# Sample attention in steps of three: a sequence's two page halves, then its caches, with the first two steps' pages loaded one stage earlier

## The chip, the cores and the metric

The program runs on one core of a Trainium2 chip. The metric is the device time of one execution in microseconds (us), here the median of three runs. Engines are named as in the profile: PE (TensorE, the matmuls), PEld (its weight loads), DVE (VectorE), ACT (ScalarE), POOL (GpSimd) and SP (SyncE). SP and POOL issue the transfers of the stages looked at here. A line such as L1074 is a line of the kernel before.

## What is computed

One layer of a hybrid decoder, for 1024 prompt rows and for 8 sequences of 8 new tokens each. The new tokens attend in two ways, and this part is what the change touches:

```python
def sample_layer(x, kva_bufs, kvb_pool, page_table, conv_buf, lw):
    ...
    for g in range(N_GROUPS):                       # windows (128,1), (512,4), (2048,16)
        buf = kva_bufs[g]
        ...
        full = jnp.concatenate([buf.astype(new_rows.dtype), new_rows], axis=1)
        groups.append((full[:, :, 0], full[:, :, 1], lg + jnp.arange(Sd, dtype=jnp.int32)))
    o_a = dilated_mixture(qa, groups)               # softmax over the cached window rows
    past = kvb_pool[page_table].reshape(B, past_len, 2, H_B, HEAD_DIM)
    full_b = jnp.concatenate([past.astype(new_kvb.dtype), new_kvb], axis=1)
    o_b = stick_breaking_block(qb, pos, full_b[:, :, 0], full_b[:, :, 1], k_pos, sb_bias)
```

Stick-breaking weighs key s by sigmoid(z_s) times the product of (1 - sigmoid(z_j)) over the later keys j, in log space: a suffix sum. It reads 32 pages of 128 rows for each sequence (keys and values, 256 KB a page), through a page table. The dilated part reads three window caches, 13 blocks of 128 rows for each sequence.

## The kernel before

The program is a chain of stages, each a block in which every engine runs its own instruction list, joined by semaphores: norm, input projection, dilated attention of the prompt, stick-breaking of the prompt (`prompt_stick_stage`), `sample_stage`, projections, FFN, final norm. Between two blocks all engines meet.

`sample_stage` runs 24 steps. Steps 0 to 15 are **stick steps**, two for each sequence: half 1 and half 0 of its pages, 16 pages each. Steps 16 to 23 are **cache steps**, one for each sequence, 13 blocks. Pages and caches land in four slots of 16 blocks. `load_pages` issues them: SP the groups 0 and 1 of each step, POOL the groups 2 and 3. A page costs a register load from the table and one transfer of 256 KB; a cache group is one transfer of up to 1 MB. The load for step k waits until step k-4 has used its slot (`v_done`).

SP's list in this stage: the page table, the 64 new rows (into `kt`, named `rows`), bias, sb_bias, two masks `own` and `own01`, `new_v`, fold, after, same, mask, three small `vnew` loads, and then its page loads. DVE's list begins with a wait for `own_in` (the last of its four transfers is `new_v`), after which a chain over DVE, ACT and PE prepares the new tokens' rows (`new_rows` on PE). PE turns the first page only behind that chain.

A step k in the list of PE: `turn(k+1)` (transposes of the next step's key blocks into the bank `tbank`, copied out to `kt` by ACT and DVE in turns), a small matmul (`carry`, or `turn_maxima` in a cache step), `turn_weights(k)`, `scores(k+1)`, in some steps a turn-out of a finished sequence (`turn_out` for stick results, L1485 and L1487, or `turn_out_shared` for cache results, L1495 and L1496), and `values(k)` (L1458), which needs `awT`, DVE's copy of the turned weights (`move_weights`, L1282). The results of a turn-out lie in the bank `xbank`; DVE puts them in their place by `place` (four small copies, L1300) or `place_shared` (a reciprocal, L1304, and four products, L1309).

Where these stand decides the waits. In the stick steps 3, 5, ... 15 PE has a `turn_out` between `scores(k+1)` and `values(k)`, and DVE has `read_out(k-1)`, which waits for it, `carried`, `place` and only then `move_weights(k)`. In the other stick steps there is none. In the cache steps DVE's `move_weights` stands ahead of `place` and `place_shared`. The order is written out by hand.

Of the kernel before, what the change touches and what calls it, by code (L numbers as in the profile page):

```python
# [20 lines left out]
P = 128  # L21
# [19 lines left out]
EPS = 1e-6  # L41
Z_MAX = 41.0
# [739 lines left out]
def prompt_stick_stage(nc, K, a, zs, oTd, extra_pool):  # L782


    with stage(nc, "ps") as s:
# [38 lines left out]
        @block.sync  # L824
        def _(sp):
            sp.dma_start(strict[:, :], a["strict"]).then_inc(small_in, 16)
            sp.dma_start(bias[:, :], a["sb_bias"].partition_broadcast(P)).then_inc(small_in, 16)
            for t in range(QT):
                sp.dma_start(rows[:, t, :], zs[t * P:t * P + P, QB:ZC]).then_inc(row_in[t], 16)
            sp.wait_ge(o_done, N)  # L830
            sp.dma_start(oTd[:, 2:4, 0:SEQ], oT[:, :, :]).then_inc(o_stored, 16)
            sp.wait_ge(o_stored, 16)

        @block.gpsimd
        def _(pool):
            for t in range(QT):
                pool.wait_ge(row_in[t], 16)
            extra_pool(pool)
# [171 lines left out]
def sample_stage(nc, K, a, zs, oTd):  # L1010


    with stage(nc, "sm") as s:
        C = 4 * NS
        HALF = PAGES // 2
        SLOTS = 4
        STICK = 2 * NB
        STEPS = STICK + NB
        ROUNDS = STEPS // SLOTS
        pages = s.sb("pages", [P, SLOTS * HALF, 512])  # L1020
        table = s.sb("table", [1, NB * PAGES], I32)
# [10 lines left out]
        out = s.sb("out", [P, 2, 256])  # L1032
# [10 lines left out]
        page_in = [[s.sem(f"page_in{u}{g}") for g in range(4)] for u in range(SLOTS)]  # L1043
        rows_in, table_in, small_in, own_in, vnew_in = (s.sem(n) for n in ("rows_in", "table_in", "small_in", "own_in", "vnew_in"))
# [13 lines left out]

        def landed(k, g):

            return sum(64 if i < STICK else 16 for i in range(k % SLOTS, k + 1, SLOTS))

        def load_pages(eng, groups):

            for k in range(STEPS):
                u = k % SLOTS
                if k >= SLOTS:
                    eng.wait_ge(v_done, k - SLOTS + 1)
                for g in groups:
                    if k < STICK:  # L1070
                        b, first = k // 2, HALF * (1 - k % 2)
                        with eng.Fori(0, 4) as j:
                            page = eng.value_load(table[0:1, ds(j + (b * PAGES + first + 4 * g), 1)], min_val=0, max_val=NPOOL - 1)
                            eng.dma_start(pages[:, ds(j + (u * HALF + 4 * g), 1), :],  # L1074
                                          a["pool"][ds(page, 1), :, :].rearrange("a p c -> p a c")).then_inc(page_in[u][g], 16)
                    else:
                        b = k - STICK
                        src = (a["cache2"][b].rearrange("(k r) c -> k r c", r=4),
                               a["cache3"][b].rearrange("(k r) c -> k r c", r=16)[:, 0:4, :],
                               a["cache3"][b].rearrange("(k r) c -> k r c", r=16)[:, 4:8, :],  # L1080
                               a["cache1"][b].unsqueeze(1))[g]
                        first = u * HALF + 4 * g
                        eng.dma_start(pages[:, first:first + (4 if g < 3 else 1), :], src).then_inc(page_in[u][g], 16)

        @block.sync
        def _(sp):
            sp.dma_start(table[:, :], a["page_table"]).then_inc(table_in, 16)
            sp.dma_start(rows[:, 0:ZC], zs[SEQ:ROWS, :]).then_inc(rows_in, 16)
            sp.dma_start(bias[:, :], a["stick_bias"]).then_inc(small_in, 16)
# [11 lines left out]
            sp.wait_ge(table_in, 16)  # L1101
            load_pages(sp, (0, 1))
# [6 lines left out]
        def _(pool):  # L1109
            pool.wait_ge(table_in, 16)  # L1110
            load_pages(pool, (2, 3))

        def move(eng, k, e):

            u = e % 2
            n = 512 if k < STICK or e < 6 else P
# [10 lines left out]
        def _(act):  # L1127
# [11 lines left out]
            for k in range(STEPS):  # L1139
                u, more = k % 2, k + 1 < STEPS  # L1140
                if k < STICK:
# [4 lines left out]
                    act.wait_ge(odds_done, k + 1)  # L1146
                    if k >= 2:
                        act.wait_ge(scanned, k - 1)
                    act.activation(soft[:, u, :], odds[:, u, :], ACT.Ln, bias=1.0).then_inc(soft_done, 1)
                    if more:  # L1150
                        move(act, k + 1, 2)
                    act.wait_ge(scanned, k + 1)
                    if k >= 2:
                        act.wait_ge(a_done, k - 1)
                    act.activation(left[:, u, :], suffix[:, u, :], ACT.Exp, scale=-1.0).then_inc(left_done, 1)
# [3 lines left out]
                    act.wait_ge(nbias_done, k + 1)  # L1159
                    act.wait_ge(o_done, max(0, k - 1))  # L1160
                    act.activation(factor[:, u:u + 1], nbias[:, u:u + 1], ACT.Exp).then_inc(factor_done, 1)
                else:
                    if more:
                        move(act, k + 1, 0)
                    act.wait_ge(nm_done, k - STICK + 1)
                    if k >= STICK + 2:
                        act.wait_ge(share_done, k - STICK - 1)
                    act.activation(odds[:, u, :], odds[:, u, :], ACT.Exp, bias=nm[:, u:u + 1], scale=SCALE,
# [855 lines left out]
```

## Time and profile before

| what | us |
| --- | --- |
| runs | 2311.25, 2316.29, 2320.03 (median 2316.29) |
| the profiled execution | 2309.15, of which its span 2307.6 |
| prompt stick-breaking, last transfer issued | 850.55 |
| sample stage, SP's first transfer issued | 855.49 |
| sample stage, first page turned on PE | 880.03 |
| sample stage, SP's first store issued | 1194.34 |

Over the whole span PE is busy 85%, DVE 42%, ACT 25%, POOL 5%. The stage of interest is some 340 us of 2308. In a timeline row the columns are: start, length, engine, line, operation, what it writes <- what it reads, shapes, count, and in brackets how long the engine sat idle before it and what released it. In a windows row they are: the stretch and its length, then for each engine its busy time with the number of instructions, and last the clock granted to TensorE (1.00 is 2.4 GHz, 0.50 is 1.2 GHz), the mean busy share of the 16 DMA engines, and GB/s.

### The profile page before, as it was taken

To read this page: it belongs to the slowest core of one execution; us is meant where nothing else is said; L and a number is where in the kernel's file an instruction comes from. 1 tells how busy PE (TensorE), PEld (TensorE's weight loads), DVE (VectorE), ACT (ScalarE), POOL (GpSimd) and SP (SyncE) were. 2 spreads that over 40 slices of the span, in tenths; PEclk is the share of its full clock that TensorE was granted. 3 is DMA by queue.
4 is the path that set the end of the run, shared out by engine and by line. 5 is a ranking of instruction groups with operands and counts; after the bars stand their busy time and mean duration, and the time that the engine had idled before them with its cause. 6 is when DMAs were issued, how large, how long until landed. Compare 5 with 4: busy or idle time off the path is not lost. (4 is left out here: it accounts for less than half of the span.)

```text
span 2307.6 us, 32275 instructions
## 1 busy us (share of the span) xinstructions
PE 1952.0 (85%) x11654; PEld 1644.0 (71%) x11654; DVE 978.0 (42%) x1841; ACT 587.2 (25%) x948; POOL 114.9 (5%) x208
## 2 busy tenths in 40 slices
PE   2799999998776747787867695799999999999984
PEld 2577888998444534555647584799999999999973
DVE  3344100000464844445436414345545455555554
ACT  3101111111754642233211103222221222122212
POOL 0000000000201003331000000000000000000000
PEclk9899999999878777999988797899999999999997
DMA  2844455111826129998633400311110111101102
GB/s 93 325 153 154 153 206 197 55 48 57 229 48 206 38 55 345 343 318 317 258 132 124 180 1 10 89 39 55 55 36 18 55 55 40 45 24 55 36 16 86
DMA packets 132446, 273.96 MB, mean 119 GB/s; under 512 B 23225, under 2 KB 74826, under 8 KB 128330
## 3 DMA queue, kind: packets, MB, share of 16 engines
q1 hardware_dynamic: 110890, 153.93, 20.0%
q0 software_dynamic: 21472, 118.91, 14.6%
q8 instruction: 53, 0.87, 0.2%
q14 instruction: 31, 0.25, 0.0%
HBM read 243.37 MB, written 79.10 MB: 140 GB/s over the span
## 5 line engine op out<-in xcount | busy, mean ns | idle before, releaser
L447 PE MATMUL ff_ups<-act_hi,ff_up_hi 128*128 128x364 f32 (+1 forms) x1056 | 234.1, 330 | 14.8 <-DVE ff_up_lo L1786 14.8
L447 PE MATMUL ff_ups<-act_lo,ff_up_hi 128*128 128x364 f32 (+1 forms) x1056 | 233.8, 330 | 0.0
L447 PE MATMUL ff_ups<-act_hi,ff_up_lo 128*128 128x364 f32 (+1 forms) x1056 | 233.8, 330 | 0.0
L1837 DVE TENSOR_TENSOR act_x<-act_x,ff_dps 128x512 f32<-128x512 f32 (+1 forms) x198 | 135.9, 686 | 216.1 <-PE ff_dps L1888 216.1
L447 PEld LDWEIGHTS ff_ups<-act_hi,ff_up_hi 128*128 128x128 f32 x1056 | 184.4, 189 | 16.5 <-DVE ff_up_lo L1786 15.0
L422 PE MATMUL inp_ps<-inp_w_hi,h_hi 128*128 (+1 forms) x432 | 170.5, 395 | 22.8 <-DVE inp_w_lo L381 20.9
L447 PEld LDWEIGHTS ff_ups<-act_lo,ff_up_hi 128*128 128x128 f32 x1056 | 184.0, 189 | 0.0
L447 PEld LDWEIGHTS ff_ups<-act_hi,ff_up_lo 128*128 128x128 f32 x1056 | 184.0, 189 | 0.0
L422 PE MATMUL inp_ps<-inp_w_lo,h_hi 128*128 (+1 forms) x432 | 170.0, 393 | 0.0
L422 PE MATMUL inp_ps<-inp_w_hi,h_lo 128*128 (+1 forms) x432 | 169.6, 393 | 0.0
L1888 PE MATMUL ff_dps<-ff_dn_hi,ff_f_hi 128*128 128x512 f32 (+1 forms) x396 | 158.0, 399 | 9.3 <-DVE ff_f_lo L1827 9.3
L1888 PE MATMUL ff_dps<-ff_dn_lo,ff_f_hi 128*128 128x512 f32 (+1 forms) x396 | 157.8, 398 | 0.0
L1888 PE MATMUL ff_dps<-ff_dn_hi,ff_f_lo 128*128 128x512 f32 (+1 forms) x396 | 157.6, 398 | 0.0
L381 DVE TENSOR_TENSOR inp_w_lo<-inp_raw,inp_w_hi (+1 forms) x10 | 44.3, 4425 | 252.3 <-ACT inp_w_hi L347 252.3
L1382 PE MATMUL sm_tbank<-all_ident,sm_pages 128*128 128x128 f32 x720 | 115.7, 299 | 35.6 <-ACT sm_kt L1122 15.9
L1382 PEld LDWEIGHTS sm_tbank<-all_ident,sm_pages 128*128 128x128 f32 x720 | 83.5, 150 | 74.4 <-issue 42.5
L422 PEld LDWEIGHTS inp_ps<-inp_w_hi,h_hi 128*128 128x128 f32 (+1 forms) x432 | 79.5, 184 | 43.3 <-issue 23.4
L1743 ACT ACTIVATE ff_c<-ff_ups,ff_cb,ff_cw 128x728 f32<-128x728 f32 x44 | 42.3, 961 | 260.5 <-PE ff_ups L447 260.5
L1756 ACT ACTIVATE ff_f_hi<-ff_c 128x1088 fp32r<-128x1088 f32 x22 | 24.5, 1114 | 305.6 <-DVE ff_c L1825 305.6
L1124 DVE COPY sm_kt<-sm_tbank 128x512 f32<-128x512 f32 x96 | 62.9, 655 | 89.2 <-PE sm_tbank L1382 89.1
L422 PEld LDWEIGHTS inp_ps<-inp_w_hi,h_lo 128*128 128x128 f32 (+1 forms) x432 | 79.6, 184 | 20.0
L422 PEld LDWEIGHTS inp_ps<-inp_w_lo,h_hi 128*128 128x128 f32 (+1 forms) x432 | 79.7, 184 | 19.8
(250 smaller groups left out, 3200.3 us busy)
## 6 DMA issues: line engine op xcount, KB each, us to landing
sm_pages<-in_pool POOLq DMA_DIRECT2D x128, 256.0 KB, 4.8
sm_pages<-in_pool SPq DMA_DIRECT2D x128, 256.0 KB, 4.6
out_s<-in_cache POOLq DMA_DIRECT2D x8, 4080.0 KB, 20.9
ff_up_raw<-in_w_up SPq DMA_DIRECT2D x44, 512.0 KB, 4.7
inp_raw<-in_w_in POOLq DMA_DIRECT2D x10, 2048.0 KB, 9.4
sm_pages<-in_cache SPq DMA_DIRECT2D x16, 1024.0 KB, 9.5
zs<-inp_zt SPq DMA_DIRECT2D x48, 256.0 KB, 4.5
ff_dn_raw<-in_w_down SPq DMA_DIRECT2D x22, 512.0 KB, 4.4
```

The source lines that it names most:

```text
L381: dve.tensor_tensor(w_lo[:, c % 2, :, :], raw[:, c % 2, :, :], w_hi[:, c % 2, :, :].bitcast(F32), ALU.subtract).then_inc(lo_done, 1)
L422: last = pe.matmul(zbank[t % 3][0:n, :], h[:, k, t * P:t * P + n], w[:, c % 2, k, :], start=(i == 0), stop=(i == 3 * KD - 1))
L447: last = pe.matmul(out[:, n * 512:n * 512 + b - a], lhs, rhs[:, a:b], start=(i == 0), stop=(i == len(pairs) - 1))
L1124: eng.tensor_copy(dst, src).then_inc(moved[1], 1)
L1382: last = pe.transpose(tbank[:, hp * 512 + j * P:hp * 512 + j * P + P], pages[:, k % SLOTS * HALF + 4 * g + j, hp * P:hp * P + P], K["ident ...
L1743: act.activation(pieces(c[:, k, 0:FRONT]), front(u), ACT.Identity, bias=cb[:, ds(j + k * FT, 1)], scale=cw[:, 2, ds(j + k * FT, 1)]).then_ ...
L1756: act.activation(f_hi[:, u, :], c[:, 1, :], ACT.Copy).then_inc(f_hi_done, 1)
L1837: dve.tensor_tensor(x, x, dps[0:n, k * 512:k * 512 + 512], ALU.add).then_inc(added, 1)
L1888: last = pe.matmul(dps[0:n, k * 512:k * 512 + 512], x[:, u, t * P:t * P + n], w[:, u, k * 512:k * 512 + 512], start=(q == 0), stop=(q == 5))
```

## The change

The 24 steps are put in another order: step 3b and 3b+1 are the two page halves of sequence b, step 3b+2 its caches. All indices follow (`stick(k)` counts stick steps). `load_pages` becomes a function of its own. The first half of the slots and the page table are allocated ahead of the prompt's stick-breaking stage, and that stage's SP and POOL issue the loads of steps 0 and 1, once its own rows are in; on POOL they stand ahead of the cache copies (`extra_pool`). In the sample stage SP issues the loads of steps 2 and 3 directly behind the new rows, ahead of the small loads. `out` has three slots instead of two. `place(b-1)` and `place_shared(b-1)` run in the stick steps 3b and 3b+1, ahead of `move_weights(k)`, and `turn_out(b-1)` and `turn_out_shared(b-1)` in the same two steps on PE.

```diff
 def prompt_stick_stage(...): sp
             for t in range(QT):
                 sp.dma_start(rows[:, t, :], zs[t * P:t * P + P, QB:ZC]).then_inc(row_in[t], 16)
+            sp.dma_start(G["table"][:, :], a["page_table"]).then_inc(G["table_in"], 16)
+            sp.wait_ge(row_in[QT - 1], 16)
+            sp.wait_ge(G["table_in"], 16)
+            load_pages(sp, G, a, (0, 1), 0, 2)
             sp.wait_ge(o_done, N)
...
             for t in range(QT):
                 pool.wait_ge(row_in[t], 16)
+            pool.wait_ge(G["table_in"], 16)
+            load_pages(pool, G, a, (2, 3), 0, 2)
             extra_pool(pool)
...
 def sample_stage(...): sp
-            sp.dma_start(table[:, :], a["page_table"]).then_inc(table_in, 16)
             sp.dma_start(rows[:, 0:ZC], zs[SEQ:ROWS, :]).then_inc(rows_in, 16)
+            load_pages(sp, G, a, (0, 1), 2, SLOTS)
             sp.dma_start(bias[:, :], a["stick_bias"]).then_inc(small_in, 16)
...
-            sp.wait_ge(table_in, 16)
-            load_pages(sp, (0, 1))
+            load_pages(sp, G, a, (0, 1), SLOTS, STEPS, v_done)
...
             def read_out(k):
...
-                dve.wait_ge(x_ready, min(k // 2, NB) + max(0, k - STICK - 1))
+                if b:
+                    dve.wait_ge(x_ready, 2 * b - 1 if is_stick(k) else 2 * b)
...
                     carried(k)
-                    if k % 2 == 1 and k >= 3:
-                        place(k // 2 - 1)
+                    if k >= 3:
+                        (place if k % 3 == 0 else place_shared)(k // 3 - 1)
                     move_weights(k)
...
                     tops(k)
                     move_weights(k)
-                    if k == STICK:
-                        place(NB - 1)
-                    if k >= STICK + 2:
-                        place_shared(k - STICK - 2)
                     peaks(k)
...
                 if k + 1 < STEPS:
                     scores(k + 1)
-                if k < STICK:
-                    if k % 2 == 1 and k >= 3:
-                        turn_out(k // 2 - 1)
-                else:
-                    if k == STICK:
-                        turn_out(NB - 1)
-                    if k >= STICK + 2:
-                        turn_out_shared(k - STICK - 2)
+                if k >= 3 and is_stick(k):
+                    (turn_out if k % 3 == 0 else turn_out_shared)(k // 3 - 1)
+                if not is_stick(k):
                     spread_tops(k)
+                if k + 1 == STEPS:
+                    turn_out(NB - 1)
                 values(k)
```

SP at the start of the sample stage, before (`sm_kt` is where the new rows land; the page loads begin behind mask and vnew).

```order
L1087 DMA sm_table<-in_page_table 1x256
L1088 DMA sm_kt<-zs 64x3072
L1089 DMA sm_bias<-in_stick_bias 128x1
L1090 DMA sm_bias4<-in_sb_bias 128x4
L1091 DMA sm_own<-in_own 64x256
L1092 DMA sm_own01<-in_own01 64x256
L1093 DMA sm_new_v<-zs 64x256
L1094 DMA sm_fold<-in_fold 128x32
```

The same place with the change. The load of a page is the body of a loop that runs four times, and the loop stands there twice, for groups 0 and 1.

```order
L1102 DMA sm_kt<-zs 64x3072
L1037 DMA sm_pages<-in_cache2 128x2048
L1037 DMA sm_pages<-in_cache3 128x2048
...
L1028 TENSOR_LOAD pg_table
...
L1029 DMA sm_pages<-in_pool 128x512
...
L1104 DMA sm_bias<-in_stick_bias 128x1
L1105 DMA sm_bias4<-in_sb_bias 128x4
L1106 DMA sm_own<-in_own 64x256
L1107 DMA sm_own01<-in_own01 64x256
L1108 DMA sm_new_v<-zs 64x256
```

Two 1 MB and eight 256 KB transfers, the eight with a register load each, now stand ahead of bias, own and new_v.

DVE from one step's last copy to `kt` to the next step's first, in two successive stick steps before: one with `place` ahead of the copy to `awT`, one without.

```order
L1124 COPY sm_kt<-sm_tbank 128x512 x2
L1292 TENSOR_SCALAR sm_out<-sm_obank,sm_factor 128x256
L1244 SCALAR_TENSOR_TENSOR sm_nbias<-sm_ybank,sm_total 128x1
L1300 COPY sm_oT<-sm_xbank 64x8 x4
L1282 COPY sm_awT<-sm_abank 128x512
L1221 TENSOR_SCALAR sm_odds<-sm_zbank,sm_bias_z 128x512
...
L1244 SCALAR_TENSOR_TENSOR sm_nbias<-sm_ybank,sm_total 128x1
L1282 COPY sm_awT<-sm_abank 128x512
```

The same with the change, in the two stick steps of a sequence.

```order
L1314 TENSOR_TENSOR sm_share<-sm_den,sm_factor 128x1
L1315 TENSOR_SCALAR sm_out<-sm_obank,sm_factor 128x256
L1262 SCALAR_TENSOR_TENSOR sm_nbias<-sm_ybank,sm_total 128x1
L1323 COPY sm_oT<-sm_xbank 64x8 x4
L1303 COPY sm_awT<-sm_abank 128x512
L1239 TENSOR_SCALAR sm_odds<-sm_zbank,sm_bias_z 128x512
...
L1262 SCALAR_TENSOR_TENSOR sm_nbias<-sm_ybank,sm_total 128x1
L1327 RECIPROCAL sm_parts<-sm_xbank 128x32
L1332 TENSOR_TENSOR sm_oT_a<-sm_xbank,sm_parts 64x8 x4
L1303 COPY sm_awT<-sm_abank 128x512
```

Both stick steps of a sequence now have work on `xbank` ahead of the copy to `awT`: 14 steps (3, 4, 6, 7, ... 21, 22) where it was 7.

## Rows read from the trace of the kernel before

**Rows 1.** Windows, two stretches of the sample stage: first page turned to step 15, then cache steps.

```profile
880.00:1077.00 197.00, 157.57 (x1338) 103.24 (x1338) 96.05 (x168) 60.82 (x116) 62.23 (x116) 0.92 0.95 331
1077.00:1195.00 118.00, 100.31 (x1222) 69.03 (x1214) 57.17 (x168) 29.82 (x68) 7.43 (x14) 0.98 0.52 204
```

**Rows 2.** Waits, 880 to 1075 us: engine, tile, line, releaser: total us, times, longest.

```profile
PE sm_tbank L1382 <- DMA sm_pages<-in_pool: 6.4, 4, 2.3
```

**Rows 3.** Timeline, start, first turned page, first values and end of the sample stage.

```profile
855.86 0.50 SPq L1088 DMA_DIRECT2D sm_kt<-zs  x1
858.68 0.60 SPq L1093 DMA_DIRECT2D sm_new_v<-zs  x1
863.92 0.18 DVE L1182 COPY sm_bias_c<-sm_bias 128x32 f32<-128x32 f32 x1 [6.16 <-DMA sm_new_v<-zs]
880.03 6.36 PE L1382 MATMUL sm_tbank<-all_ident,sm_pages 128*128 128x128 f32 x28 [0.26 <-DVE sm_total L1211]
...
899.08 1.94 PE L1458 MATMUL sm_obank<-sm_pages,sm_awT 128*32 128x256 f32 x32
...
1193.56 0.75 DVE L1309 TENSOR_TENSOR sm_oT_a<-sm_xbank,sm_parts 64x8 f32<-64x8 f32 x4
```

**Rows 4.** Timeline, SP's first page loads.

```profile
863.99 7.96 SPq L1074 DMA_DIRECT2D sm_pages<-in_pool  x6
```

**Rows 5.** DMA issues by line: count, KB each, median us from issue to landing.

```profile
sm_pages<-in_cache SPq DMA_DIRECT2D x16, 1024.0 KB, 9.5
```

**Rows 6.** Timeline of PE, stick steps 7 and 8 (values of 6, 7, 8).

```profile
979.03 1.94 PE L1458 MATMUL sm_obank<-sm_pages,sm_awT 128*32 128x256 f32 x32
980.89 1.09 PE L1382 MATMUL sm_tbank<-all_ident,sm_pages 128*128 128x128 f32 x8
...
988.19 1.92 PE L1395 MATMUL sm_zbank<-sm_kt,sm_qpad 128*32 128x512 f32 x16
...
991.27 0.63 PE L1487 MATMUL sm_xbank<-sm_fold,sm_out 128*128 128x32 f32 x4
994.12 2.73 PE L1458 MATMUL sm_obank<-sm_pages,sm_awT 128*32 128x256 f32 x32 [2.21 <-DVE sm_awT L1282]
...
1006.24 1.94 PE L1458 MATMUL sm_obank<-sm_pages,sm_awT 128*32 128x256 f32 x32
```

**Rows 7.** Values of line 1458: idle time before them, us and times.

```profile
  DVE sm_awT L1282: 15.5, 7
```

**Rows 8.** Timeline of DVE, end of step 7: from the turn-out's landing to awT.

```profile
992.05 0.48 DVE L1292 TENSOR_SCALAR sm_out<-sm_obank,sm_factor 128x256 f32<-128x256 f32 x1 [3.96 <-PE sm_xbank L1487]
...
992.51 0.74 DVE L1300 COPY sm_oT<-sm_xbank 64x8 f32<-64x8 f32 x4
993.28 0.69 DVE L1282 COPY sm_awT<-sm_abank 128x512 f32<-128x512 f32 x1
```

**Rows 9.** Timeline of DVE, `place_shared` in a cache step.

```profile
1148.24 0.36 DVE L1304 RECIPROCAL sm_parts<-sm_xbank 128x32 f32<-128x32 f32 x1 [1.76 <-PE sm_xbank L1496]
1148.63 0.75 DVE L1309 TENSOR_TENSOR sm_oT_a<-sm_xbank,sm_parts 64x8 f32<-64x8 f32 x4
```

**Rows 10.** Timeline of PE, a cache step: values, turn of the next, turn-out.

```profile
1148.44 2.07 PE L1458 MATMUL sm_obank<-sm_pages,sm_awT 128*32 128x256 f32 x32
...
1151.09 1.09 PE L1382 MATMUL sm_tbank<-all_ident,sm_pages 128*128 128x128 f32 x8
...
1156.01 0.27 PE L1435 MATMUL sm_ybank<-all_ident,sm_mx 128*1 128x128 f32 x1
...
1159.33 0.39 PE L1496 MATMUL sm_xbank<-sm_fold,sm_share 128*128 128x32 f32 x2
...
1159.95 2.07 PE L1458 MATMUL sm_obank<-sm_pages,sm_awT 128*32 128x256 f32 x32
```

**Rows 11.** Windows around step 7's wait for awT: ahead of it, just behind it.

```profile
980.00:992.00 12.00, 10.20 (x88) 6.70 (x80) 4.56 (x7) 3.95 (x7) 4.23 (x8) 1.00 0.98 352
995.00:998.00 3.00, 3.00 (x26) 1.90 (x19) 0.00 (x0) 0.07 (x1) 0.48 (x1) 0.52 0.91 303
```

More of the change, by code:

```diff
@@ L41 @@
 EPS = 1e-6
+SLOTS = 4
 Z_MAX = 41.0
@@ L1007, in _, with load_pages, sample_stage @@
                     values(it - 1, turns[it - 1] - 1)
-def sample_stage(nc, K, a, zs, oTd):
+def load_pages(eng, G, a, groups, first, last, consumed=None):
+    for k in range(first, last):
+        u, half = k % SLOTS, k % 2 * (PAGES // 2)
+        pages = G["pages"][u // 2]
+        if k >= SLOTS:
+            eng.wait_ge(consumed, k - SLOTS + 1)
+        for g in groups:
+            if k % 3 < 2:
+                at = k // 3 * PAGES + PAGES // 2 * (1 - k % 3) + 4 * g
+                with eng.Fori(0, 4) as j:
+                    page = eng.value_load(G["table"][0:1, ds(j + at, 1)], min_val=0, max_val=NPOOL - 1)
+                    eng.dma_start(pages[:, ds(j + (half + 4 * g), 1), :],
+                                  a["pool"][ds(page, 1), :, :].rearrange("a p c -> p a c")).then_inc(G["page_in"][u][g], 16)
+            else:
+                b = k // 3
+                src = (a["cache2"][b].rearrange("(k r) c -> k r c", r=4),
+                       a["cache3"][b].rearrange("(k r) c -> k r c", r=16)[:, 0:4, :],
+                       a["cache3"][b].rearrange("(k r) c -> k r c", r=16)[:, 4:8, :],
+                       a["cache1"][b].unsqueeze(1))[g]
+                eng.dma_start(pages[:, half + 4 * g:half + 4 * g + (4 if g < 3 else 1), :], src).then_inc(G["page_in"][u][g], 16)
+def sample_stage(nc, K, G, a, zs, oTd):
     with stage(nc, "sm") as s:
@@ L1057, in sample_stage, with is_stick, stick, page @@
         block = s.ctx.enter_context(nc.Block())
+        def is_stick(k):
+            return k % 3 < 2
+        def stick(k):
+            return k // 3 * 2 + k % 3
         def landed(k, g):
[L1061 to L1069, printed above, removed]
-                    if k < STICK:
[L1071 to L1075, printed above, removed]
-                    else:
[L1077 to L1083, printed above, removed]
+            return sum(64 if is_stick(i) else 16 for i in range(k % SLOTS, k + 1, SLOTS))
+        def page(k, i):
+            return G["pages"][k % SLOTS // 2][:, k % 2 * HALF + i, :]
         @block.sync
         def _(sp):
-            sp.dma_start(table[:, :], a["page_table"]).then_inc(table_in, 16)
             sp.dma_start(rows[:, 0:ZC], zs[SEQ:ROWS, :]).then_inc(rows_in, 16)
+            load_pages(sp, G, a, (0, 1), 2, SLOTS)
             sp.dma_start(bias[:, :], a["stick_bias"]).then_inc(small_in, 16)
@@ L1140, in _ @@
                 u, more = k % 2, k + 1 < STEPS
-                if k < STICK:
+                if is_stick(k):
+                    m = stick(k)
+                    v = m % 2
                     if more:
@@ L1459, in add @@
                                      tile_position=(row, C * g), skip_group_check=True)
-                if k < STICK:
+                if is_stick(k):
                     for j in range(4):
                         for g in range(4):
-                            last = add(g, awT[:, u, j, C * g:C * g + C], pages[:, page + 4 * g + j, 256:512], j == 0, j == 3)
+                            last = add(g, awT[:, u, j, C * g:C * g + C], page(k, 4 * g + j)[:, 256:512], j == 0, j == 3)
                 else:
-                    if k == STICK:
+                    b = k // 3
+                    if b == 0:
                         pe.wait_ge(vnew_in, 48)
@@ L1955, in program @@
         prompt_dilated_stage(nc, K, a, o, zs, scratch["ls"], oTd)
-        prompt_stick_stage(nc, K, a, zs, oTd, lambda pool: copy_caches(pool, a, o, copied, (0, 1)))
-        sample_stage(nc, K, a, zs, oTd)
+        with ExitStack() as c1:
+            s1 = Store(nc, c1, "pg")
+            G = {"pages": [s1.sb("pages", [P, PAGES, 512])], "table": s1.sb("table", [1, NB * PAGES], I32), "table_in": s1.sem("table_in"),
+                 "page_in": [[s1.sem(f"page_in{u}{g}") for g in range(4)] for u in range(SLOTS)]}
+            prompt_stick_stage(nc, K, G, a, zs, oTd, lambda pool: copy_caches(pool, a, o, copied, (0, 1)))
+            sample_stage(nc, K, G, a, zs, oTd)
         with ExitStack() as c1:
```

192 lines of the change are left out of this document (95 added, 97 removed).

## The prediction

> **What bounds the kernel now.** I read the windows of the sample stage first, since the change lies there. While page halves are worked on, the DMA engines are 95% busy at 331 GB/s; in the cache steps they are half idle (52%, 204 GB/s) [rows 1]. Read alone, this speaks for mixing the two kinds of step. The waits say otherwise: in that first stretch of 197 us PE waited for a page 4 times, 6.4 us in all [rows 2]. A full DMA queue is not yet a late one. The timeline of PE shows what sets the pace: values, turn, scores, turn-out and values again follow with small gaps, 979.03 to 994.12 to 1006.24 [rows 6]. The rest is PE's own list and the copies that it waits for.
>
> The start must be read next, as the change loads two steps ahead of it. SP issues the new rows at 855.86 and new_v at 858.68; DVE goes on at 863.92, released by new_v; the chain behind it ends at 880.03, when PE turns the first page, released by DVE's copy of the totals and not by a page [rows 3]. So **the first step's pages were in time already**. Loading them earlier gives PE nothing. What counts at the start is when new_v lands.
>
> **Part 1: the loads issued a stage earlier.** They go out after that stage's own rows are in; SP's next work there is the store at the stage's end, and POOL's only other work is the cache copies, which nobody awaits until the program's end. 32 page transfers of 256 KB are 8.4 MB, 25 us at 331 GB/s [rows 1], inside a stage with over 100 us left (850.55 is its last transfer). I cost them at nothing; if they disturbed it, a few us.
>
> **Part 2: the small loads behind the loads of steps 2 and 3.** SP's page loads come at (7.96 - 0.35) / 5 = 1.52 us apart, six in 7.96 us [rows 4] (0.35 is about one issue's own time). Ahead of new_v there are now eight of them, 12.2 us, and two cache transfers, some 0.4 us each, less the page table's, which has gone (0.37): it is issued about **12.6 us later**, at 871.3 instead of 858.68 [rows 3]. Then it must land, which took 863.92 - 858.68 = 5.2 us [rows 3]. Now SP and POOL have put the loads of steps 2 and 3 into the queues from 857 on, 3.4 MB of caches and 4.2 MB of pages, all issued by 870; at 331 GB/s [rows 1] these 7.6 MB drain at 857 + 23 = 880. A 1 MB cache transfer, issued together with others, landed after 9.5 us [rows 5], which from 871.3 gives 880.8. If new_v lands only behind SP's own loads, DVE goes on at about 880.5: **+16.6 us**. Bounds: +12.6 if it passes them all, +21 if the small ones ahead of it add 4 us. I take 16.6, since more than half of the backlog (4.2 of 7.6 MB) is on SP's own queue. The chain behind it keeps its 880.03 - 863.92 = 16.1 us; mask, fold and same are needed only 12 us into it. PE starts to turn at 896.6.
>
> The Trainium skill, page "DMA: Bandwidth & Descriptors", section "Queues, rings and completion order", says that a DMA engine takes turns between the queues it has work for and takes the descriptors of one queue in order. By that rule a small transfer on SP's queue cannot pass SP's pages, whatever POOL has queued, which is the 16.6; by overtaking the sum would be 4.0 us less. No row of the trace before has a small transfer behind a backlog.
>
> While PE waits, all four slots are full, so the DMA engines stand idle from 880 until step 0's values free one, at 896.6 + 19.05 (899.08 - 880.03, [rows 3]) = 915.6. They have time to spare, see below.
>
> **Part 3: place ahead of awT in 14 steps instead of 7.** In step 7 the turn-out ends at 991.90 and values start at 994.12: PE sat idle 2.21 us because DVE, released by the turn-out, did out, nbias, place and awT first [rows 6, 8]. This is paid 7 times, 15.5 us [rows 7]. With the change read_out asks for an older turn-out, so out and nbias (992.05 to 992.51, 0.46) go ahead of it: a wait of 2.21 - 0.46 = 1.75 in the first stick step of each sequence. In the second, place_shared takes 1148.24 to about 1149.40, 1.16 us, instead of place's 993.28 - 992.51 = 0.77 [rows 8, 9]: 1.75 + 0.39 = 2.14. Seven of each: 7 x 1.75 + 7 x 2.14 = 27.2. Less 15.5: **+11.7 us**. In the cache steps PE did not wait for place_shared before, since awT stood ahead of it: its values start at 1159.95 right behind the turn-out [rows 10], so nothing comes back there.
>
> **Part 4: the turn of page halves in cache steps.** PE's matmuls are the same in number and shape, only in another order. In a cache step, the turn of 13 blocks took 1156.01 - 1151.09 = 4.9 us for 26 transposes [rows 10]; in a stick step 32 of them with carry and weights took 988.19 - 980.89 = 7.3 [rows 6]. The sums over the stage stay as they were within about **+1.5 us** (the last copy to kt of a half now has only the turned weights of a cache step to hide behind, 0.2 us in 7 steps). The bounds are 0 and 3.
>
> **Part 5: waits for pages.** These 6.4 us [rows 2] go: **-6.4 us** at most, -3 where they hid other gaps. A sequence asks for 2 x 4.2 + 3.4 = 11.8 MB in three steps. PE needs for these, by [rows 6, 10], 15.1 + 14 + 10.4, some 39.5 us; the transfers need 11.8 MB / 331 GB/s = 35.6 us. So pages stay in time, with a small margin.
>
> **Part 6: TensorE's clock.** Behind step 7's wait the granted clock was 0.52 (1.2 GHz), against 1.00 ahead of it, and values took 2.73 us instead of 1.94 [rows 6, 11]. From there to the next values it is 1006.24 - 994.12 = 12.1 us, where the parts at full clock give 1.86 (values) + 7.30 (turn and weights) + 1.9 (scores) = 11.1 [rows 6]: a fall costs about 1.1 us. The mean clock of that stretch, 0.92, means half speed for 16% of 197 us [rows 1]; looked at in windows of 2 us, five of the 7 waits have such a spell right behind them. I take the same share of 14, 10 falls, 5 more: **+5.5 us**. Bounds: -5.5 if the shorter waits trip nothing, +9.9 if each does.
>
> The page "TensorE: Matmul & The Clock Gate", section "A second HAM failure mode: psum-queue depth-cycling", of the Trainium skill describes short idle times between groups of matmuls that are frequent enough to make the clock go back and forth. The rows agree at 2.21 us of idle; by that rule doubling such gaps costs the 5.5, without it the sum would be 5.5 less.
>
> **The sum.** 16.6 + 11.7 + 1.5 - 6.4 + 5.5 = **+28.9 us**, slower. On the profiled execution, 2309.15, that is 2338.1. This execution was 7.1 us below the median of the runs, 2316.29; against the median it is 2345.2, and I say 2345. The unknown terms at their low ends: 12.6 + 11.7 + 0 - 6.4 - 5.5 = +12.4; at their high ends 21 + 11.7 + 3 - 3 + 9.9 = +42.6.
>
> **Rivals.** (a) **Pages are the bound after all**, and the result is faster. If the pace of the stick steps follows the traffic (95% busy, [rows 1]) and PE's small gaps hide it, then taking 8.4 MB out of the stage saves 25 us and spreading the rest fills the idle half of the cache steps; with the start's loss of 16.6 and 11.7 of Part 3 hidden in the slack, the time is some 2292 to 2305. It decides from the point where PE's waits for pages exceed the 29 us of the other terms; against it stand the 6.4 us [rows 2]. (b) **new_v does not wait**, and the clock does not fall more often: +12 or a little less, 2324 to 2329; within 0.5% if DVE, which starts its next step right behind awT, gives back part of Part 3. For it: the transfer is small; against it: 12.6 us of issue alone are sure. (c) **Pages run late**: cache transfers of 1 MB and pages share three steps of 39.5 us with 35.6 us of transfers. If the rate falls to 300 GB/s, these need 39.4, and waits of 1 to 3 us in each of 7 sequences come on top: 2355 to 2366. (d) **The early loads do not run early**: POOL or SP issue them late in the prompt's stage. Since the first turn waits for the chain and not for pages, this changes nothing.
>
> **How the numbers follow.** Forecast, +18 to +40: 0.68. (b) 0.16, half of it within 0.5% of the time before. (c) 0.08. (a) 0.08, three quarters of it faster by over 0.5%. 0.5%, 11.6 us, is about what a measurement of this kernel can tell from no change. So faster 0.06, within 0.5% 0.11, slower 0.83. The range of 8 in 10 goes from 2324 (the low ends together, 2328.7, and 4 for the spread of the runs) to 2361 (the high ends together, 2358.9, and part of (c)).
>
> **What would show it.** In the timeline after: DVE's bias_c released by new_v at about 880 instead of 863.9; the first turn 16 us behind that, released by DVE; a DMA share near nothing between 880 and 915. In the idle times ahead of values: 14 waits for awT, 27 us. In the waits: none of note for pages. In the windows: clock falls behind most of the 14. Wrong would be: new_v landed by 872; a stage shorter than 339 us; long waits of PE for pages, which would be (c).

## The result

The changed kernel takes 2361.93 us (median of 4 runs, 2359.70 to 2364.09); beside it the kernel before took 2314.62 (4 runs, 2311.25 to 2320.03). The ratio is 1.0202, interval 1.0178 to 1.0226: 2% slower. The direction was forecast, the size was not: 2345 was said, with a range up to 2361, and the measured time lies just above that.

### The profile after

The profiled execution took 2364.09 us, its span 2362.6: 55.0 more than before. Windows of the sample stage after: from SP's first transfer to the end of the chain that prepares the new rows, then from there to SP's first store. The columns are those of [rows 1].

```profile
858.81:901.25 42.44, 8.62 (x38) 6.30 (x38) 8.84 (x27) 2.95 (x5) 5.42 (x10) 0.50 0.64 217
901.25:1251.39 350.14, 280.62 (x2552) 175.50 (x2552) 153.76 (x337) 90.36 (x184) 63.41 (x118) 0.89 0.64 225
```

The same two stretches of the kernel before:

```profile
855.49:879.81 24.32, 8.62 (x38) 6.30 (x38) 8.85 (x27) 2.95 (x5) 7.79 (x14) 0.50 0.98 291
879.81:1194.34 314.53, 257.88 (x2552) 172.27 (x2552) 153.38 (x337) 90.64 (x184) 69.66 (x130) 0.94 0.79 284
```

I call the first the start, the second the compute stretch. They account for the 55.0 us:

| where | before | after | us |
| --- | --- | --- | --- |
| up to the prompt stage's last transfer | 850.55 | 853.81 | +3.3 |
| start | 24.32 | 42.44 | +18.1 |
| compute stretch, PE busy | 257.88 | 280.62 | +22.7 |
| compute stretch, PE idle | 56.65 | 69.52 | +12.9 |
| the rest | | | -2.0 |

The largest row is not a wait. PE ran the same 2552 matmuls in both and was busy with them 22.7 us longer, at a granted clock of 0.89 instead of 0.94. At half speed for a share s of a stretch the mean clock is 1 - s/2, so 0.89 means some 77 us at 1.2 GHz of the 350, and 0.94 some 38 us of the 315 (counted in windows of 1 us: 77 in 22 spells, and 35 in 9).

The +3.3 is not shown to come from the change. Of all thirteen kernels profiled, the ten with the early loads issued that last transfer between 849.6 and 856.2, the three without (before, e5, e7) at 850.6 to 852.2.

**The start.** SP after; answers to the first two rows of [rows 3]:

```profile
858.81 0.53 SPq L1102 DMA_DIRECT2D sm_kt<-zs  x1
861.45 10.84 SPq L1029 DMA_DIRECT2D sm_pages<-in_pool  x8
875.61 1.62 SPq L1108 DMA_DIRECT2D sm_new_v<-zs  x1
```

DVE after, in the same stretch:

```profile
885.36 0.18 DVE L1200 COPY sm_bias_c<-sm_bias 128x32 f32<-128x32 f32 x1 [24.28 <-DMA sm_new_v<-zs]
901.25 0.17 DVE L1229 COPY sm_total<-sm_ybank 128x8 f32<-128x8 f32 x1 [3.60 <-PE sm_ybank L1387]
```

new_v is issued 16.8 us behind SP's first transfer, where it was 3.2 ([rows 3] and the table ahead of the prediction), and lands 885.36 - 875.61 = 9.8 us later instead of 5.2. PE waits with DVE: it is idle 23.5 us ahead of its first matmul behind this, where it was 4.9.

**The compute stretch.** What PE's values waited for after, which answers to [rows 7]:

```profile
  DVE sm_awT L1303: 25.9, 14
```

PE after: the values of a sequence's first stick step, then its second, in which the blocks of the cache step are turned and scored:

```profile
1042.92 3.57 PE L1478 MATMUL sm_obank<-pg_pages,sm_awT 128*32 128x256 f32 x32 [1.66 <-DVE sm_awT L1303]
1046.42 1.09 PE L1401 MATMUL sm_tbank<-all_ident,sm_pages 128*128 128x128 f32 x8
...
1050.79 0.96 PE L1401 MATMUL sm_tbank<-all_ident,sm_pages 128*128 128x128 f32 x5 [0.64 <-DVE sm_kt L1137]
1052.23 0.33 PE L1401 MATMUL sm_tbank<-all_ident,sm_pages 128*128 128x128 f32 x1 [0.48 <-DVE sm_kt L1137]
...
1053.92 1.08 PE L1422 MATMUL sm_zbank<-sm_kt,sm_qpad 128*32 128x256 f32 x8
```

Windows over the same stretch:

```profile
1039.00:1043.00 4.00, 2.34 (x23) 1.74 (x20) 1.57 (x6) 0.00 (x0) 1.61 (x3) 0.98 1.02 343
1043.00:1046.50 3.50, 3.50 (x33) 1.58 (x34) 0.44 (x1) 0.00 (x0) 0.02 (x1) 0.53 0.74 274
1046.50:1053.00 6.50, 4.47 (x32) 3.37 (x33) 4.23 (x7) 3.63 (x7) 2.07 (x4) 1.00 0.63 193
1053.00:1056.50 3.50, 3.50 (x48) 2.13 (x50) 0.34 (x2) 0.20 (x1) 1.15 (x3) 0.52 0.89 303
```

There are two kinds of spell. The first follows a wait for awT: clock 0.53, and values take 3.57 us instead of the 1.94 of [rows 6]. The second follows no such wait. It comes at the end of the turn of a cache step's 13 blocks, whose last group has one transpose for each copy (the `x1` row) instead of four, and it lies on the scores of the caches, where one group of 8 takes 1.08 us. From the third sequence on, each has three spells of some 3.5 us. All 14 waits for awT are followed by one (values take 2.76 to 3.60 us), and 6 of the 8 thin ends. Before, 5 of the 7 waits were, though all seven lasted 2.21 us; and the second kind came once, at the change from stick to cache steps, with the same row at 1.08 us (in the other seven cache steps it took 0.61):

```profile
1096.29 1.08 PE L1404 MATMUL sm_zbank<-sm_kt,sm_qpad 128*32 128x256 f32 x8
```

The idle time of the compute stretch grew by 12.9 us. Waits for awT account for +10.4 and waits for pages for -6.4. What is left is small and frequent: waits of the turn for the copies to `kt`, 28.7 us before and 35.9 after, and short issue gaps ahead of the scores, 1.5 and 3.5 us. The waits for the copies, before and after:

```profile
PE sm_tbank L1382 <- ACT sm_kt L1122: 15.9, 46, 0.6
PE sm_tbank L1382 <- DVE sm_kt L1124: 12.8, 36, 0.6
```

```profile
PE sm_tbank L1401 <- ACT sm_kt L1135: 20.6, 53, 0.6
PE sm_tbank L1401 <- DVE sm_kt L1137: 15.3, 32, 0.6
```

### The profile page after: what moved, and what is told of

Its sections match the earlier page's. It is cut to its first block and busy times, and to the rows that moved or that the text cites. A ratio compares the mean times of both kernels' runs of the same rounds, so it can differ in the third digit from the quotient of the medians.

```text
span 2362.6 us, 32273 instructions
## 1 busy us (share of the span) xinstructions
PE 1974.9 (84%) x11654; PEld 1644.4 (70%) x11654; DVE 979.9 (41%) x1841; ACT 587.1 (25%) x948; POOL 115.1 (5%) x208
## 5 line engine op out<-in xcount | busy, mean ns | idle before, releaser
L382 DVE TENSOR_TENSOR inp_w_lo<-inp_raw,inp_w_hi (+1 forms) x10 | 44.3, 4426 | 252.4 <-ACT inp_w_hi L348 252.4
L1135 ACT ACTIVATE sm_kt<-sm_tbank 128x512 f32<-128x512 f32 x96 | 54.3, 565 | 186.7 <-PE sm_tbank L1401 186.0
L1904 PEld LDWEIGHTS ff_dps<-ff_dn_hi,ff_f_hi 128*128 128x128 f32 (+1 forms) x396 | 72.7, 184 | 29.1 <-DVE ff_f_lo L1843 9.7
```

Source lines behind the costliest of these rows:

```text
L382: dve.tensor_tensor(w_lo[:, c % 2, :, :], raw[:, c % 2, :, :], w_hi[:, c % 2, :, :].bitcast(F32), ALU.subtract).then_inc(lo_done, 1)
L1135: eng.activation(dst, src, ACT.Copy).then_inc(moved[0], 1)
L1904: last = pe.matmul(dps[0:n, k * 512:k * 512 + 512], x[:, u, t * P:t * P + n], w[:, u, k * 512:k * 512 + 512], start=(q == 0), stop=(q == 5))
```

## The experiments

The theory: three independent costs, namely the small loads behind the pages; the waits for awT with the clock falls behind them; and the clock falls at the thin end of a cache turn, now between page halves in every sequence (this third one was added after e1 to e8). Rivals: the traffic of pages and caches, the order in threes by itself, and for the clock, that more work for PE lowers it. Unless said otherwise an experiment is an edit of the changed kernel. "Start" and "compute stretch" are as above.

**e1_small_first** puts the loads of steps 2 and 3 on SP back behind the small loads.

```diff
             sp.dma_start(rows[:, 0:ZC], zs[SEQ:ROWS, :]).then_inc(rows_in, 16)
-            load_pages(sp, G, a, (0, 1), 2, SLOTS)
...
-            load_pages(sp, G, a, (0, 1), SLOTS, STEPS, v_done)
+            load_pages(sp, G, a, (0, 1), 2, STEPS, v_done)
```

> The changed kernel with one edit: SP issues the loads of steps 2 and 3 behind the small loads again. Theory (new_v behind SP's page loads, 18.1 us of the 57 that the sample stage ends later, and a term of its own): new_v lands some 5 us after its issue, the first page is turned about 24.5 us after SP's first transfer of the stage instead of 42.7, and the time falls by 16 to 19 us, to about 2344. Rival (POOL's loads of steps 2 and 3, which stay early, hold the small loads as well, or the pages of steps 2 and 3 are then late): it falls by under 8 us, with waits for pages in steps 2 and 3.

Measured: 2350.66 us, ratio to before 1.0152 (1.0130 to 1.0174). That is 11.3 less than after and short of what was expected: the start is 29.4 us, where the kernel before has 24.3. SP's new_v, issued at 859.82 with none of SP's pages ahead of it, landed 10.5 us later. The first row is DVE's, the second POOL's, which began with its share of the loads at once:

```profile
870.32 0.18 DVE L1199 COPY sm_bias_c<-sm_bias 128x32 f32<-128x32 f32 x1 [11.23 <-DMA sm_new_v<-zs]
```

```profile
857.30 1.10 POOL L1037 DMA_DIRECT2D sm_pages<-in_cache  x2 [96.26 <-POOLq L142]
```

So order on SP's own queue is one part of it, POOL's queue another.

**e6_pool_held** asks for that second part. It is e3 (below, both edits) with POOL's page loads held until new_v is in.

```diff
+            pool.wait_ge(own_in, 64)
             load_pages(pool, G, a, (2, 3), 2, STEPS, v_done)
```

> The kernel of e3, in which POOL waits for the small loads (own_in) before it loads steps 2 and 3. In e3 the small loads landed 13.6 us after SP's first transfer of the stage, before it was 8.4. Theory (POOL's two cache transfers and pages on the same DMA engines hold them): new_v lands at 8 to 9 us, and the time falls by 5 us, to about 2299. Rival (something else delays them, or steps 2 and 3 come late): no change, or waits for pages in step 2.

Measured: 2298.49 us, 0.9908 (0.9891 to 0.9924), against 2304.01 of e3. The start is 24.1 us instead of 29.4; new_v, issued at 859.68, is in at 864.64, as in the kernel before:

```profile
864.91 1.10 POOL L1037 DMA_DIRECT2D sm_pages<-in_cache  x2 [108.95 <-DMA sm_new_v<-zs]
```

POOL's loads on their own cost the start 5.3 us. e5 (below) narrows it down to the two 1 MB cache transfers at their head.

**e2_awt_first** takes away the wait for awT: DVE copies awT ahead of `place` and `place_shared`.

```diff
                     carried(k)
+                    move_weights(k)
                     if k >= 3:
                         (place if k % 3 == 0 else place_shared)(k // 3 - 1)
-                    move_weights(k)
```

> The changed kernel with one edit: DVE copies awT before place and place_shared in the stick steps. Theory A (each of the 14 waits for awT costs its 1.85 us and, behind it, a spell of half clock of about 1.65 us): the waits (25.9 us in all) go, the spells behind them go too, and the time falls by 26 + 23 = some 45 to 50 us. Theory B (the spells come from the small gaps of the turns and stay where they are): it falls by 22 to 28 us, and values still run at half clock in most of the stick steps.

Measured: 2314.83 us, 0.9991 (0.9977 to 1.0006): 47.1 less than after, the same as before. The compute stretch:

```profile
903.85:1202.43 298.58, 254.00 (x2552) 165.68 (x2552) 153.93 (x337) 90.31 (x184) 63.21 (x118) 0.96 0.74 264
```

It lost 51.6 us, 26.6 of it PE's busy time with the same 2552 matmuls, 25.0 idle time. PE never waits for awT, and the values of the stick steps run at full speed, as here:

```profile
1043.67 1.93 PE L1478 MATMUL sm_obank<-sm_pages,sm_awT 128*32 128x256 f32 x32
```

The small work of `place` or `place_shared` ahead of awT, 14 times, cost half in waiting and half in the clock behind it. Low clock fell from 77 us to 23.

**e3_both** has both edits.

> The changed kernel with both edits of the two runs before. If the terms are independent, its gain is the sum of the two: under theory A some 60 to 68 us, which is below the kernel before (about 2297); under B some 42 us, to about 2320, the kernel before within 0.5%. If one hides the other (pages then late, since PE is faster), it is less than the sum, with waits for pages.

Measured: 2304.01 us, 0.9947 (0.9928 to 0.9965): 57.9 less than after, where 11.3 + 47.1 = 58.4. By the medians the two costs add, though short of the 60 to 68 that was expected, and the close agreement is in part chance: the compute stretch was 306.6 us here and 298.6 in e2, with low clock of 41 and 23 us, though both run the same lists in it. Two of the spells in e3 lasted some 10 us each, where none in e2 did (the one at the start apart, all lasted 3 to 4). How long the clock stays low differs between near copies by so much, and what decides it there I can't say.

**e4_filler** leaves the wait and fills it: 11 transposes of the identity on PE, nobody's input, stand behind each turn-out of the stick steps. If the clock follows PE's gaps, values run at full speed though DVE is as late as before.

```diff
                 if k >= 3 and is_stick(k):
                     (turn_out if k % 3 == 0 else turn_out_shared)(k // 3 - 1)
+                    for _ in range(11):
+                        pe.transpose(tbank[:, 0:P], K["ident"][:, :], K["ident"][:, :])
```

> The changed kernel with more work for PE: in the 14 steps that have a turn-out, 11 transposes of the identity into a bank that nobody reads, 1.5 us at full clock, between the turn-out and values, where PE waits for awT. Its results are unchanged. Theory A (the wait itself makes the clock fall): PE no longer stands idle there, values run at full clock, and the time FALLS, by 14 x 1.65 = up to 23 us, although work was added. Theory B (the fall has another cause): values stay at half speed, the filler itself takes up to 3 us at half clock, and the time stays or grows by up to 15 us.

Measured: 2346.58 us, 1.0139 (1.0109 to 1.0169). **154 useless matmuls made the kernel 15.4 us faster** (by the medians; 14.6 by the ratios to the kernel before; up to 23 was expected). The same place as above, PE:

```profile
1037.83 1.40 PE L1536 MATMUL sm_tbank<-all_ident 128*128 128x128 f32 x11
1039.64 1.93 PE L1478 MATMUL sm_obank<-pg_pages,sm_awT 128*32 128x256 f32 x32 [0.42 <-DVE sm_awT L1303]
...
1049.46 1.08 PE L1422 MATMUL sm_zbank<-sm_kt,sm_qpad 128*32 128x256 f32 x8
```

The values behind the turn-out take 1.93 or 1.94 us again, 13 times of 14; the one exception (2.04 us) lies at the end of a spell of 10 us that began at a thin turn. The second kind of spell is left. So it is PE's idle time there, not the copy or the traffic, that costs the clock, and more work does not lower it. Whether the length of the gap counts or the share of busy time around it, the filler doesn't tell, since it changes both. The compute stretch:

```profile
900.67:1232.38 331.71, 279.74 (x2706) 189.09 (x2706) 153.95 (x337) 90.23 (x184) 63.21 (x118) 0.94 0.67 238
```

**e9_padded_turn** is e6 with the thin end filled: three transposes of the identity ahead of the single one in the last group of a cache step, so that each group has four again.

```diff
+                    if not is_stick(k) and g == 3:
+                        for j in range(1, 4):
+                            pe.transpose(tbank[:, hp * 512 + j * P:hp * 512 + j * P + P], K["ident"][:, :], K["ident"][:, :])
                     for j in range(4 if is_stick(k) or g < 3 else 1):
```

> The kernel of e6 (three-step order, awT first, small loads first, POOL held) with more work for PE: in the turn of a cache step's 13 blocks, whose last group has one transpose where the others have four, three transposes of the identity are added on each side, 6 x 0.14 us for each of 8 sequences, 6.7 us in all. Results are unchanged. In e2, e5 and the changed kernel a spell of half clock begins once a sequence at the end of just this turn and lies on the cache scores behind it. Theory (the thin end of this turn is what lets the clock fall, and the order in threes puts it under a stick step 8 times where it was once): low-clock time in the stage goes from some 40 us to about 20, the compute stretch loses 9 us by it and gains 2 to 7 by the added work: 0 to 8 us faster than e6's 2298.5 in spite of the work. Rival (the spells have another cause): low-clock time stays, and the time grows by 3 to 8 us.

**e11_filler_and_padded_turn** puts both fillings into the changed kernel, small loads and waits left as they are.

> The changed kernel with the filler of e4 (11 transposes in each of the 14 waits for awT) and the padding of e9 in the cache turns. Theory: the two causes of the spells are then both gone, low-clock time in the stage goes from 77 us (e4: 38) to about 20, and the time to 2338 to 2346, at or below e4's 2346.6 in spite of 6.7 us more work. Rival: low-clock time stays at e4's 38 us and the time is 3 to 7 us above e4's.

Measured, e9: 2288.40 us, 0.9886 (0.9867 to 0.9905); e6 was 2298.49 at 0.9908. By the ratios that is 5 us, with intervals that overlap; the evidence is in the profiles. Compute stretch, first e6, then e9:

```profile
880.98:1187.83 306.85, 262.29 (x2552) 170.34 (x2552) 153.85 (x337) 90.23 (x184) 63.22 (x118) 0.93 0.74 263
```

```profile
880.71:1174.18 293.47, 251.33 (x2600) 165.90 (x2600) 153.74 (x337) 90.22 (x184) 63.21 (x118) 0.99 0.78 275
```

48 matmuls more, PE busy 11.0 us less, low clock from 41 us to 7, where 20 was expected. Measured, e11: 2335.47 us, 1.0089 (1.0069 to 1.0109), 11.1 less than e4, clock 0.99 in a stretch of 319.2, low clock 5 us in one spell. So the second kind of spell is the thin turn's, and it is worth 11 us to a kernel that has it in each sequence. With both fillings the changed kernel is 26.5 us faster, although DVE is as late with awT as before; of the 25.9 us of waits for it, 8.7 are left, and PE turns the identity during the rest.

**e5_no_early_load** is e3 without the loads in the prompt's stage; SP and POOL load steps 0 and 1 in the sample stage.

> The kernel of e3 (three-step order, small loads first, awT first) without the early loads: steps 0 and 1 are loaded in the sample stage, as in the kernel before. Theory (the first page turned waits for the chain behind new_v, so early pages give nothing): within 3 us of e3's 2304.0, the chain beginning 1 to 5 us earlier since POOL then starts with pages instead of a 1 MB transfer, against 3 to 6 us of waits for pages in the first steps. Rival (the early load is worth the 25 us of traffic that it takes out of the stage, and e3 wins by it): some 15 to 25 us slower than e3, 2319 to 2329.

Measured: 2303.67 us, 0.9939 (0.9922 to 0.9956), e3's 2304.01 at 0.9947. The early loads gain e3 nothing: its compute stretch is the same within 0.4 us, and its start is 29.4 us where it is 24.1 here. One page was late:

```profile
PE sm_tbank L1398 <- DMA pg_pages<-in_pool: 3.5, 1, 3.5
```

The shorter start is instructive, since POOL is not held here. It begins with single pages and not with two cache transfers, and new_v, issued at 859.95, lands after 5.4 us:

```profile
858.82 0.56 POOL L1027 DMA_DIRECT2D pg_pages<-in_pool  x1 [127.45 <-issue]
865.35 0.23 DVE L1197 COPY sm_bias_c<-sm_bias 128x32 f32<-128x32 f32 x1 [5.95 <-DMA sm_new_v<-zs]
```

Against e6, whose start is also 24.1, the medians give the early loads 5.2 us. That is not shown: the intervals overlap, the compute stretches agree within 0.1, and the profiled executions are 0.4 us apart.

**e8_small_loads_early** is e3 with bias4, own, own01 and new_v loaded in the prompt's stage behind its pages, and POOL held by the new rows only. The question is what bounds the start next.

> The kernel of e3 with new_v, own, own01 and sb_bias loaded in the prompt's stick-breaking stage, and POOL's loads of steps 2 and 3 held until the new rows are in. Theory (the start is bound by when the chain's inputs land): DVE goes on at the landing of the new rows and their turn, about 8.5 us after SP's first transfer instead of 13.6, and the time falls by 5 us against e3, to about 2299. Rival: the chain then waits for something else, no change.

Measured: 2294.91 us, 0.9915 (0.9888 to 0.9941), not told apart from e6. DVE takes bias_c 2.2 us behind SP's first transfer, and nothing is gained on e6, because the turned new rows are next, 8.4 us behind it, as forecast:

```profile
863.12 4.02 DVE L1208 COPY sm_qpad<-sm_tbank 64x64 f32<-64x64 f32 x16 [6.08 <-PE sm_tbank L1375]
```

**e7_old_order_awt_first** and **e10_old_order_early_load** start from the kernel before, order of steps unchanged. e7 gives `out` four slots, lets read_out ask for an older turn-out, and copies awT ahead of `place`. e10 is e7 with the early loads of steps 0 and 1, and POOL held until new_v is in.

```diff
-                dve.wait_ge(x_ready, min(k // 2, NB) + max(0, k - STICK - 1))
+                dve.wait_ge(x_ready, max(0, k // 2 - 1) if k < STICK else NB + max(0, k - STICK - 1))
...
                     carried(k)
+                    move_weights(k)
                     if k % 2 == 1 and k >= 3:
                         place(k // 2 - 1)
-                    move_weights(k)
```

> The kernel before (16 stick steps, then 8 cache steps, no early loads) with the awT edit alone: out has four slots, read_out asks for an older turn-out, and awT stands ahead of place. Theory (the 7 waits of 2.21 us and the spells of half clock behind 5 of them are dead time in the old order too): 15.5 + 5 x 1.1 to 1.6 = 21 to 24 us faster than before, about 2294, and so faster than e3: the order in threes gives nothing of itself. Rival (the old order's stick steps are bound by pages at 95% DMA, once PE stops waiting for awT): waits for pages take the place of it, the gain is under 10 us, and e3 is the faster of the two.

> The kernel of e7 (old order, awT first) with the early loads of the changed kernel: steps 0 and 1 loaded in the prompt's stick-breaking stage, POOL held until the small loads are in. e7 is the one kernel here in which PE waits for pages (10.8 us in 5 waits), so here the early load may be worth something. Theory: the waits go in full or in part, the start stays at 24.2 us: 4 to 10 us faster than e7's 2290.0. Rival (the 16 stick steps in a row drain the two steps' lead, and the waits only come later; or the prompt's stage pays for it): no change, within 3 us.

Measured, e7: 2290.02 us, 0.9886 (0.9860 to 0.9912): 26 us faster than the kernel before by the ratio, where 21 to 24 were expected, and 13.6 less than e5, the nearest kernel in threes. Compute stretch of e5, then of e7, and e7's waits for pages:

```profile
881.23:1188.14 306.91, 260.39 (x2552) 170.41 (x2552) 154.09 (x337) 90.35 (x184) 69.11 (x129) 0.94 0.82 291
```

```profile
880.48:1174.86 294.38, 248.51 (x2552) 167.25 (x2552) 153.55 (x337) 90.79 (x184) 69.64 (x130) 0.97 0.83 304
...
PE sm_tbank L1382 <- DMA sm_pages<-in_pool: 10.8, 5, 2.7
```

PE is idle 46.5 us in the one and 45.9 in the other. Nearly the whole difference is busy time, 11.9 us, so what the order in threes costs is clock; that it is by the thin turns is argued from e9, where filling them gave back 11.0. The idle times are equal because two things cancel: e5 waits 7.3 us less for pages, but 5.9 more for the copies to `kt` (35.2 and 29.3) and 2.0 more in issue gaps.

Measured, e10: **2280.72 us**, 0.9856 (0.9831 to 0.9881), faster than both kernels and the fastest of the study. No wait for a page is left, and low clock is 7 us. Against e7 the compute stretch lost 7.2 us, 4.5 of it idle time: 10.8 us of page waits went, and 5.7 came back as waits for the copies to `kt` (35.0 and 29.3):

```profile
880.52:1167.71 287.19, 245.78 (x2552) 163.46 (x2552) 152.90 (x337) 90.33 (x184) 63.25 (x118) 0.99 0.77 285
```

At this clock PE's matmuls take 245.8 us in the old order; in threes (e9) 251.3 less its 48 padding matmuls, some 0.13 us each (11 took 1.40 on their own), makes 245.2. So the same work costs the same in either order. Measured from there, the kernel before loses 12 us of busy time to the clock, the changed kernel 35.

## Why the forecast was right in direction and wrong in size

**Part 1 (early loads, 0).** For the changed kernel, right: first turn behind the chain and not behind a page, and e5 equals e3. As a general statement too narrow: where PE waits for pages they take these waits away, 7.2 us of the compute stretch in e10 against e7. They did run early, from 725.9 us on, as forecast.

**Part 2 (small loads, +16.6).** 18.1 measured. Issue was 13.6 us later by the trace, not 12.6: the small issues ahead of it got slower (the one of L1106 takes 1.56 us instead of 0.49). Landing added 4.5 against 4.0. The reason given was half wrong. I took SP's own backlog as what new_v lands behind; e1 shows that POOL's alone delays it by as much, 10.5 us against 5.0 in e6, and e5, with single pages at the head of POOL's list, 5.4. The Trainium skill, page "DMA: Bandwidth & Descriptors", section "Queues, rings and completion order", has the engines take turns between queues, which I read as a small transfer passing POOL's. In e1 it did not pass them unharmed. Moving SP's loads back (e1) took 13.1 of the 18.1 off the start, holding POOL's (e6 against e3) the other 5.3.

**Part 3 (awT, +11.7).** Right: 25.9 us in 14 waits where 27.2 were forecast, +10.4.

**Part 4 (the turn in cache steps, 0 to +3).** About right in its own terms: of two kernels that wait neither for awT nor for a page, the one in the old order (e10) is idle 41.4 us in the compute stretch and the one in threes (e6) 44.6. Its mechanism was looked at for lateness only. The row of one transpose per copy was in [rows 10]'s stage of the trace and was counted as cheap; that it drops the clock when it stands in a stick step was not seen, though the kernel before shows it once, at 1094.

**Part 5 (pages, -6.4).** Right in that no wait for a page is left, but not worth 6.4: other gaps came in their place. In e10 against e7, 10.8 us of page waits were worth 4.5 of idle time, so the -3 named there was nearer. The 39.5 us that PE was said to need for a sequence don't follow from [rows 6, 10] either, which give 15.1, 12.1 and 11.5; after, a sequence took 44.3 us (from the values at 1042.92 to those at 1087.25), so the transfers had more room than said.

**Part 6 (clock, +5.5, at most +9.9) is the step that failed.** Measured +22.7 us of busy time. Two errors. First, how many: "the same share of 14" gave 10 spells instead of 5; there were 22 instead of 9, 14 of them behind the waits (5 before) and 6 behind thin turns (1 before). Each of the shorter waits (1.66 us) dropped the clock, while two of the seven of 2.21 us before had not. Second, how much: 1.1 us was read off one spell; 13 more of them cost 22.7, 1.7 each. With 77 us at half speed in place of 35, the loss should be up to half of 42, 21 us, which fits. With 22.7 for 5.5 the sum would have been +46.1 on the profiled execution, and the median at 2362. That this meets the measured 2361.93 is luck: the profiled executions are 55.0 us apart, 8.9 more, and the one before lay 7.1 below its median and the one after 2.2 above. The upper bound of +9.9 let each of the 14 waits trip the clock once and had no room for a spell elsewhere.

Between the forecast +28.9 and the measured +55.0 on the profiled executions, Part 6 is 17.2 us. The next is short gaps: of the 12.9 us of idle time, 10.4 are waits for awT and -6.4 pages, so 8.9 are gaps of PE for the copies to `kt` and for issue, where Part 4 had 1.5. The prompt stage ended 3.3 later, the start was 1.5 longer than said, awT 1.3 less, and the rest is -2.0.

**The rivals.** (a), pages as the bound, falls: taking page waits away gave 7.2 us of the compute stretch at the best (e10 against e7). (b), new_v doesn't wait, falls by the 9.8 us of landing. (c), pages late, falls: no such wait, although 2362 is in its range; by the time alone it would have looked right. (d) decides nothing, as said. The Trainium skill's "TensorE: Matmul & The Clock Gate", section "A second HAM failure mode: psum-queue depth-cycling", describes short idle times that send the clock to and fro. The trace agrees, and more strongly than I let it count: it was given +5.5 us, e2 shows 26.6 us of busy time that return when the waits go, and e9 11.0 when the thin turns are filled.

What stays open: why low clock was 41 us in e3 and 23 in e2 with the same lists. Executions of one kernel differ in this too: of 14 executions of the kernel before, the fastest took 2311.7 us at a mean clock of 0.921, the slowest 2324.2 at 0.913. Open is also why 2 of 7 equal waits, and 2 of 8 thin turns after, did not drop it, and whether the early loads have a part in the prompt stage's +3.3. Undoing only the order in threes of the changed kernel, with its other edits kept, was not tried.

## What to carry to other kernels

A wait of PE is paid twice when it drops the clock, once as idle time and again as half speed on the dense work behind it. Compare PE's busy time for the same matmuls, before looking at waits. When steps are put in another order, look for thin ones (one matmul per handshake) that now stand ahead of dense work. A copy that PE waits for goes first on its engine, and small loads that a chain waits for go ahead of bulk on every queue, not on their own alone.

## What the runs showed of the hardware

- Work nobody needs can make a kernel faster: 154 transposes saved 15.4 us (e4), 48 more another 11.1 (e11).
- After, a spell at 1.2 GHz lasted some 3.5 us, behind a wait of 1.66 us as behind one of 2.04 us, and also behind groups with gaps of 0.34 to 0.64 us that end in single transposes. In e3, e4, e5, e6 and e8 single spells lasted some 10 us.
- A wait for a page is worth less than it is long where it stands among short gaps: 10.8 us of them gone, 4.5 us of idle time saved (e10 against e7).
- A 64 KB transfer on SP's queue landed in 5.0 us with nothing of POOL's ahead of it (e6), in 5.4 with POOL's single pages of 256 KB 1.5 us apart (e5), in 10.5 with POOL's pages and, ahead of them, two 1 MB transfers of POOL's (e1), in 9.8 with SP's and POOL's bulk (after).
- SP's issues of small transfers took up to 1.62 us instead of 0.60 behind ten large ones.
